# Reading TensorE's weight tiles with a step of two elements, with the columns of two neighbouring tiles interleaved in memory

## What is computed

```python
def swiglu(h, wg, wu, wd):
    return (jax.nn.silu(h @ wg) * (h @ wu)) @ wd

for li in range(DEPTH):                      # DEPTH = 2
    x = x + 0.5 * swiglu(rmsnorm(x, norm_ffn1[li]), ffn1_w_gate[li], ffn1_w_up[li], ffn1_w_down[li])
    h = rmsnorm(x, norm_mix[li])
    if li % 2 == 0:
        y = even_mixer(h, ...)               # h @ w_in, two recurrences, @ w_out
    else:
        y = pool_mixer(h, ...)               # h @ w_in, windowed means, one matrix per group
    x = x + y
    x = x + 0.5 * swiglu(rmsnorm(x, norm_ffn2[li]), ffn2_w_gate[li], ffn2_w_up[li], ffn2_w_down[li])
y = rmsnorm(x, final_norm)
```

## Time and profile before

| what | value |
|---|---|
| time, median of 3 runs | 1013.05 us (1012.27 to 1013.24) |
| the profiled execution: its own time, its span | 1012.74 us, 1011.0 us |
| TensorE busy: matmuls, weight loads | 1002.0 us, 990.2 us |
| VectorE, ScalarE, GpSimd busy | 665.2 us, 510.1 us, 97.9 us |
| instructions of TensorE | 8382 loads and 8382 matmuls |
| read from memory | 171.19 MB, 176 GB/s with what is written |

### The profile page before, as it was taken

How to read it: one execution, slowest core, us unless ns; L and a number is a source line. 1 busy time by engine, 2 the same in 40 slices (tenths; PEclk the granted TensorE clock), 3 DMA queues, 4 the chain that set the end, 5 groups by cost and what they waited for, 6 DMA issues and landing times.

```text
span 1011.0 us, 21425 instructions
## 1 busy us (share of the span) xinstructions
PE 1002.0 (99%) x8382; PEld 990.2 (98%) x8382; DVE 665.2 (66%) x896; ACT 510.1 (50%) x716; POOL 97.9 (10%) x158
## 2 busy tenths in 40 slices
PE   9999999999999999999999999999999999999998
PEld 8999999999999989999999999999999999999998
DVE  6766564588887877766664495666546986666543
ACT  7544443476784646444443474444436364444334
POOL 6800000010021202000000020000001020000001
PEclk9999999999999999999999999999999999999999
DMA  7665566555453525655556556556654536556551
GB/s 255 198 204 185 183 211 206 194 169 169 145 166 115 164 80 167 207 168 183 191 177 196 179 173 211 188 170 209 190 179 144 168 126 210 167 187 191 184 186 44
DMA packets 49749, 177.90 MB, mean 176 GB/s; under 512 B 5944, under 2 KB 5960, under 8 KB 49680
## 3 DMA queue, kind: packets, MB, share of 16 engines
q1 hardware_dynamic: 46224, 165.50, 50.9%
q0 software_dynamic: 3184, 11.35, 3.7%
q10 hardware_dynamic: 288, 0.32, 0.1%
HBM read 171.19 MB, written 6.52 MB: 176 GB/s over the span
## 4 chain that ended last, share of the span: by engine, by line
PE 92%; DVE 4%; ACT 2%; issue 1%; DMA 1%; POOL 0%; SPq 0%; DVEq 0%; ACTq 0%; POOLq 0%
PE ps L1786 29%; PE ps L1787 28%; PE ps L1788 28%; PE ps L1612 1%; DVE w_lo L1253 1%; DMA raw<-in_ffn_w_gate 1%; DVE PT L1212 1%; PE ps L1622 0%; PE ps L1585 0%; ACT xw_hi L609 0%; PE ps L1652 0%; PE ps L1591 0%; POOL hn L1977 0%; ACT w_hi L599 0%; DVE xw_lo L1274 0%
## 5 line engine op out<-in xcount | busy, mean ns | idle before, releaser
L599 ACT CAST w_hi<-raw 128x1024 fp32r<-128x1024 f32 x309 | 322.5, 1049 | 413.8 <-PE ps L1788 411.8
L1253 DVE TENSOR_TENSOR w_lo<-raw,w_hi 128x1024 fp32r<-128x1024 f32 x309 | 374.8, 1229 | 183.4 <-ACT w_hi L599 182.5
L1786 PE MATMUL ps<-xw_hi,w_hi 128*128 128x264 f32 x1472 | 417.7, 284 | 1.7 <-DVE w_lo L1253 1.4
L1787 PE MATMUL ps<-xw_lo,w_hi 128*128 128x264 f32 x1472 | 416.0, 283 | 0.0
L1788 PE MATMUL ps<-xw_hi,w_lo 128*128 128x264 f32 x1472 | 416.0, 283 | 0.0
L1786 PEld LDWEIGHTS ps<-xw_hi,w_hi 128*128 128x128 f32 x1472 | 276.6, 188 | 3.8 <-DVE w_lo L1253 2.2
L1787 PEld LDWEIGHTS ps<-xw_lo,w_hi 128*128 128x128 f32 x1472 | 276.7, 188 | 0.1
L1788 PEld LDWEIGHTS ps<-xw_hi,w_lo 128*128 128x128 f32 x1472 | 276.7, 188 | 0.0
L1786 PE MATMUL ps<-a_hi,w_hi 128*128 (+1 forms) x704 | 198.9, 283 | 0.0
L1787 PE MATMUL ps<-a_lo,w_hi 128*128 (+1 forms) x704 | 198.9, 283 | 0.0
L1788 PE MATMUL ps<-a_hi,w_lo 128*128 (+1 forms) x704 | 198.9, 283 | 0.0
(11 more groups left out here) (365 smaller groups left out, 755.8 us busy)
## 6 DMA issues: line engine op xcount, KB each, us to landing
raw<-in_ffn_w_up SPq DMA_DIRECT2D x88, 512.0 KB, 4.2
raw<-in_ffn_w_down SPq DMA_DIRECT2D x88, 512.0 KB, 4.2
raw<-in_ffn_w_gate SPq DMA_DIRECT2D x87, 512.0 KB, 4.3
raw<-in_w_in_even SPq DMA_DIRECT2D x32, 512.0 KB, 3.3
raw<-in_w_out_even SPq DMA_DIRECT2D x8, 512.0 KB, 3.7
raw<-in_pool_w_in SPq DMA_DIRECT2D x8, 512.0 KB, 3.8
out<-SBUFS POOLq DMA_DIRECT2D x4, 512.0 KB, 3.5
x<-in_x SPq DMA_DIRECT2D x4, 264.0 KB, 5.2
```

Of the source, the lines that this page charges most:

```text
L599: nc.scalar.copy(w_hi[:, w % SPL, :], raw[:, w % RAW, :]).then_inc(hi_done, 1)
L1253: nc.vector.tensor_tensor(w_lo[:, w % SPL, :], raw[:, w % RAW, :], w_hi[:, w % SPL, :].bitcast(F32), ALU.subtract).then_inc(lo_done, 1)
L1786: mm(out, wh, hi, start=first, stop=False)
L1787: mm(out, wh, lo, start=False, stop=False)
```

## The change

The host interleaves the columns of each two neighbouring weight tiles (`paired`): of 256 columns, tile 0 column 0, tile 1 column 0, tile 0 column 1, and so on. This is done for all matrices that go through slots. `three` then reads a tile as 128 columns with a step of two elements, from the first or the second element of its pair of tiles. DMAs, casts, subtractions, waits and the order of all matmuls stay as they are, and so do the results.

```diff
             def three(out, s, c0, hi, lo, first, last):
 
-                wh = w_hi[:, s % SPL, c0:c0 + P]
-                wl = w_lo[:, s % SPL, c0:c0 + P]
+                c1 = c0 // BLK * BLK
+                cols = slice(c1 + c0 % BLK // P, c1 + BLK, 2)
+                wh = w_hi[:, s % SPL, cols]
+                wl = w_lo[:, s % SPL, cols]
                 mm(out, wh, hi, start=first, stop=False)
                 mm(out, wh, lo, start=False, stop=False)
                 return mm(out, wl, hi, start=False, stop=last)
...
+_PAIRED = _BLOCKED + ["ffn1_w_down", "ffn2_w_down"]
...
+def paired(w):
+
+    return w.reshape(w.shape[:-1] + (-1, 2, P)).swapaxes(-1, -2).reshape(w.shape)
...
     out["w_in_even"] = w[:, :, :16 * BLK]
+    for name in _PAIRED:
+        out[name] = paired(out[name])
     for name in _BLOCKED:
         out[name] = slots(out[name])
```

## The result

| | before | after |
|---|---|---|
| time, median of 4 runs each | 1013.04 us (1012.27 to 1013.24) | 1024.59 us (1023.8 to 1029.65) |
| ratio, 95% interval | | 1.0131 [1.010, 1.0162] |
| the profiled execution, its span | 1012.74, 1011.0 us | 1023.9, 1022.2 us |

One of the 75 runs of the kernel before that this document draws on took 1639.6 us at a granted clock of 0.56; it is left out everywhere.

A forecast was written before the change was run, and what follows sets the result against it. TensorE's stream of 7488 matmuls, 120.9 ns apart, was taken as the bound. Saving 5.9 ns each gave 1012.7 - 44.2 + 1.5 (given back in the mixer) = 970 us; whole range 950 to 1035.

The forecast's parts named there:

- The bound: Whole kernel: TensorE, busy 1002.0 of 1011.0 us; distance between starts of 7488 matmuls, mean 120.9 ns, sets the time.
- I read this as two readers, moving operand and weights, that get in each other's way: In `three`: moving-operand and weight reads at unequal speeds cause the excess of 6 to 8.6 ns; equal speeds remove it.
- 110.0 plus the 5.0 of L1612 = 115.0 ns, a gain of 5.9 x 7488 = 44.2 us: Each matmul of `three`: 264 columns at 2.4 GHz plus the overhead seen on plain f32, down from 120.9 ns.
- 111.7, a gain of 69 us: Lower bound per matmul of `three`: closest distance in ns of pairs with a 128-column load, 9.2 ns saved on each of 7488.
- 122.8 ns with x_hi: Input projection, 960 matmuls, moving rows 264 elements apart: would save 7.5 us, of which 1.5 given back for VectorE.
- tells 0.2% (2 us) from nothing: Whole kernel's time: claimed that a measurement can distinguish a change as small as 2 us from no change.
- So far the pattern doesn't matter: Weight loads: a step-0 broadcast load takes 190 ns, as does a step-1 load, so access pattern had shown no cost.
- The far end: Upper bound per matmul of `three`: stepped load reading takes twice as long, 215 ns, +704 us; nothing in the trace excluded it.
- Nothing changes: Matmuls of `three`: excess belongs to the moving operand alone, load stays hidden; 1011 to 1015 us; chance 0.18.
- The excess only takes another of its values: All matmuls of `three` run at 120.0 ns, 6.8 us less, 1006 us; chance 0.06.
- The load becomes the bound, mild: Load before each of 7488 matmuls: stepped load slows distance to 122 ns, +9 us, 1022 us; chance 0.14.
- More meetings: Weight loads in `three` touch twice the memory, doubling the 8.6 ns excess: +64 us, 1077 us; chance 0.11.

The follow-up runs named there:

- b1_steps: Bench, not the kernel: blocks of 90 f32r matmuls, varied load steps, load widths and moving columns; with 264 columns steps 1, 2, 4, 8 took 120.0, 120.0, 233.3, 241.2 ns.
- before_kick48: The kernel before plus one extra unread matmul of 48 columns in FFN 0 and one of 24 in FFN 2; median 1010.84 us, ratio 1.000.
- run 264: Not a run's label: the words say that the engine had run matmuls of 264 moving columns in b1_steps; steps 4 and 8 took 233.3 and 241.2 ns.

## Why the prediction was wrong

**The bound** was right. TensorE's stream of 7488 matmuls sets the time, the distance between starts is its measure, and ScalarE and VectorE kept their 1050 and 1229 ns and followed.

**The step that failed is "I read this as two readers, moving operand and weights, that get in each other's way"**, and with it "110.0 plus the 5.0 of L1612 = 115.0 ns, a gain of 5.9 x 7488 = 44.2 us". No stage of any kernel ran below 120.0. Where the sum had 115.0 ns, the runs showed 120.0 as the least, and the moving operand takes it by itself: 0.448 ns per column with 64-column loads, and the same 120.0 for 264 columns with loads of 128. The plain-f32 rows ask for columns at half the rate, and that is enough for them to show little excess. b1_steps agrees: where the granted clock was at its lower level, f32r matmuls with 32-column loads had none.

```profile
L145 PE MATMUL ps<-m_hi,w_hi x6: 409/422/422, 180.4 to 183.7; 128*32 128x264 f32 x6
...
core 0: us, PE busy (x) PEld busy (x) ACT busy (x) POOL busy (x), PEclk, DMA share, GB/s
...
180.50:183.50 3.00, 3.00 (x16) 2.30 (x16) 0.00 (x0) 0.00 (x0) 0.50 0.00 0
```

(183.7 - 180.4)/5/3 = 220.0 ns each, which is 264/1.2. There moving operand and weights have equal speeds too, so this alone doesn't tell the two readings apart; the short loads and the step of two at the upper clock do, which both left 120.0. So the earlier trace rows were no bound for 264 columns at the upper clock, and the end "111.7, a gain of 69 us" wasn't one either. The observation that was to carry the reading, 121.3 in FFN 0 and 120.0 in FFN 1 with equal work, was sound, but it says only that 1.3 ns of the 10.9 depend on how the stream runs. I gave the whole excess the cause of its smallest part. Two more lines of the working don't hold: of the 122.8 ns with x_hi nothing was given back either (122.8 after), and "tells 0.2% (2 us) from nothing" was too fine, as the unchanged kernel's own runs spread over 0.7%.

**"So far the pattern doesn't matter"** was wrong by little: 187 becomes 196 ns, and 111.7 becomes 117.8 where the load binds. The far end, a load of 215 ns, was named for step 2; it is what step 4 gives (233.3). By the Trainium skill (SBUF — State Buffer, Door 1) a 16-byte line must be hit at least twice for full rate, and each access that crosses to a new line pays a penalty; a step of two f32 elements hits a line twice, one of four once. The runs agree: there is a cliff between the two (117.8 and 233.3 ns), with step 3 between them at 175.6, and a step of two isn't quite free, +6.1 ns.

**The rivals.** *Nothing changes* had the 120.0 right ("264/2.2 is 120.0") and had the load hidden, which FFN 3 shows; what it missed is that 121.3 in FFN 0, noted as "against it", was a second rhythm of the same stream, and that a longer load makes this one dearer and, by the rungs, more frequent. *The excess only takes another of its values* named the right kind of thing and the wrong sign: the stream did change its rhythm, in three stages for a dearer one. Its 1006 was also out of reach, as it took the projection to 120.0 too; with all four FFNs at 120.0, before_kick48 took 1009.2. *The load becomes the bound, mild* had the direction and, by luck, the time, 1022. Its mechanism isn't what happened: the stepped load at its own pace takes 6.1 ns more than the other (117.8 against 111.7) where this rival needed 11 (from 105 to 116), so it doesn't reach 120.0, let alone 122 in every matmul; three stages stood at 123.3 and one at 120.0. *More meetings* asked for 128 ns and more; no stage came near that. If moving operand and load disturb each other at all, the runs show it in the uneven rhythm and, by 2 ns, with 496 moving columns. By the same page (Who interferes with whom) TensorE's two read ports are independent and it never waits; an extra of 1.3 ns with short-step loads, 3.3 with stepped ones and none with 64-column loads does not fit that in full.

**What stays open**: why a stream has more than one rhythm. Something in the timing of load and moving operand repeats and persists; loads of 64 columns, some offsets and some entries escape it. The runs show what changes it, not what it is. Open too is a placement or an entry that holds the even rhythm in every run; for before it would be worth 1011 - 1008.4 = 2 to 3 us.

## What to carry to other kernels

Before an excess is given to a conflict of two readers, make one of them short: a bench of a few dozen matmuls with 64-column loads showed in a few microseconds that nothing was to be had. Read distances between starts stage by stage, and where equal stages have unequal distances, suspect a rhythm of the stream, which can move by itself between runs; a change that only lengthens a hidden operation can still make the uneven one dearer. In such a stream a weight tile read with a step of two 4-byte elements cost 1.3 to 1.5% of the kernel's time and one with a step of four 83%.

## What the runs showed of the hardware

- The moving operand on f32r numbers streams at 0.448 ns per column at the upper clock (63.3 ns for 136 columns, 206.7 for 456) and at 1.2 GHz without an excess (220.0 for 264).
- The load's pace depends on its step: 111.7, 117.8, 175.6, 233.3 ns with steps 1, 2, 3, 4 at the upper clock where it binds. With step 4 it doesn't depend on TensorE's clock: 233.3 at the upper level (the block of line L133 above), and 233.3 at the lower level here, while steps 1 and 2 take 213.3 at the lower level. The clock fell within the block of 64 moving columns with step 1 that began at 102.6 us; before it the engine had run 264 moving columns with steps 4 and 8 at the upper level. Below is the window with the lower clock (PEclk 0.50), then the block with step 4, and (158.2 - 137.9)/29/3 = 233.3.

```profile
core 0: us, PE busy (x) PEld busy (x) ACT busy (x) POOL busy (x), PEclk, DMA share, GB/s
...
140.00:158.00 18.00, 18.00 (x79) 18.00 (x79) 0.00 (x0) 0.00 (x0) 0.50 0.00 0
...
L141 PE MATMUL ps<-m_hi,w_hi x30: 401/417/418, 137.9 to 158.2; 128*128 128x64 f32 x30
```

- One kernel on one core, unchanged, takes 1008.2 to 1015.1 us, a spread of 0.7% that no wait in the profile explains and that I put down to the rhythms of its four FFNs.
